# Differential attention with values by head beside queries and keys, one step less in flight, the output projection begun within it, and a first norm that is interleaved

## What is computed

```python
def diff_mixer(h, cos, sin, w_in, lam_vecs, subln_g, w_o, lambda_init):
    q, k, v = jnp.split(h @ w_in, 3, axis=-1)            # 8 heads, 2 x 64 wide; values 128 wide
    q = rope_partial(q.reshape(B, T, H, 2, dh), cos, sin) * (dh ** -0.5)
    k = rope_partial(k.reshape(B, T, H, 2, dh), cos, sin)
    lam = jnp.exp(jnp.sum(lf[0] * lf[1])) - jnp.exp(jnp.sum(lf[2] * lf[3])) + lambda_init
    for i in range(T // Q_BLOCK):                          # 4 blocks of 128 queries
        s = jnp.einsum('bhiqd,bhikd->bhiqk', qb, k[:, :, :, :L])
        p = jax.nn.softmax(jnp.where(mask, s, -jnp.inf), axis=-1)
        a = p[:, :, 0] - lam * p[:, :, 1]
        outs.append(jnp.einsum('bhqk,bhkv->bhqv', a, v[:, :, :L]))
    o = rmsnorm_2(o, subln_g) * (1.0 - lambda_init)
    return o.reshape(B, T, D_MODEL) @ w_o
```

## Time and profile before

| what | us |
|---|---|
| median of 3 runs (lowest, highest) | 2480.9 (2480.77, 2481.79) |
| the profiled execution's own time | 2478.61 |
| its span, first to last instruction | 2476.8 |
| TensorE busy in the span | 2400.5 |
| VectorE busy | 1275.1 |
| ScalarE busy | 821.8 |
| GpSimd busy | 170.0 |
| mean granted clock of TensorE | 0.982 of full speed |

### The profile page before, as it was taken

The page is one execution under the profiler, slowest core; times in us unless marked ns, Lnnn a source line. Parts: engine busy times, 40 slices in busy tenths (PEclk is TensorE's granted clock), DMA queues, the critical chain, the costliest instruction groups (busy, mean ns, idle before and its releaser), DMA issues.

```text
span 2476.8 us, 26889 instructions
## 1 busy us (share of the span) xinstructions
PE 2400.5 (97%) x10944; PEld 1913.9 (77%) x10944; DVE 1275.1 (51%) x1845; ACT 821.8 (33%) x1218; POOL 170.0 (7%) x146
## 2 busy tenths in 40 slices
PE   8999999999999999999999999999998879999998
PEld 6788887877777888887788778888776657888886
DVE  4654544476243455544543466664447773644343
ACT  3322223423433322222543343322333443423221
POOL 0000002021012000001110100000112211000001
PEclk8999999999999999999999999999999989999999
DMA  7756632311112256541232246663141102343330
GB/s 276 248 187 210 195 120 73 97 43 43 60 52 69 85 170 216 193 136 49 94 102 60 69 124 212 209 207 124 38 132 49 43 26 68 118 131 94 97 96 34
DMA packets 80793, 288.06 MB, mean 116 GB/s; under 512 B 8976, under 2 KB 9104, under 8 KB 80672
## 3 DMA queue, kind: packets, MB, share of 16 engines
q1 hardware_dynamic: 79952, 284.78, 36.1%
q10 hardware_dynamic: 720, 1.57, 0.2%
HBM read 284.22 MB, written 2.10 MB: 116 GB/s over the span
## 4 chain that ended last, share of the span: by engine, by line
PE 86%; DVE 8%; ACT 2%; issue 1%; POOL 1%; DMA 1%; SPq 1%; DVEq 0%; ACTq 0%
PE bank L279 23%; PE bank L277 23%; PE bank L278 22%; PE bank L320 2%; PE bank L322 2%; PE bank L321 2%; PE bank L360 1%; PE bank L297 1%; PE bank L302 1%; PE bank L298 1%; PE bank L389 1%; DVE dsm L1856 1%; DVE wlo L1326 1%; PE bank L367 1%; POOL h_sb L1946 1%
## 5 line engine op out<-in xcount | busy, mean ns | idle before, releaser
L1326 DVE TENSOR_TENSOR wlo<-raw,whi 128x1024 fp32r<-128x1024 f32 (+1 forms) x370 | 461.9, 1250 | 464.0 <-ACT whi L829 463.6
L277 PE MATMUL bank<-yhi,whi 128*128 128x512 f32 x1728 | 685.5, 397 | 6.8 <-DVE ylo L1428 3.7
L279 PE MATMUL bank<-yhi,wlo 128*128 128x512 f32 x1728 | 675.1, 391 | 0.0
L278 PE MATMUL bank<-ylo,whi 128*128 128x512 f32 x1728 | 675.1, 391 | 0.0
L829 ACT ACTIVATE whi<-raw 128x1024 fp32r<-128x1024 f32 (+1 forms) x370 | 384.6, 1041 | 359.6 <-PE bank L279 264.6
L277 PEld LDWEIGHTS bank<-yhi,whi 128*128 128x128 f32 x1728 | 326.3, 189 | 82.9 <-issue 10.7
L278 PEld LDWEIGHTS bank<-ylo,whi 128*128 128x128 f32 x1728 | 326.4, 189 | 69.5 <-issue 3.3
L279 PEld LDWEIGHTS bank<-yhi,wlo 128*128 128x128 f32 x1728 | 325.9, 189 | 69.2
L279 PE MATMUL bank<-mlp_ahi,wlo 128*128 128x512 f32 x512 | 204.2, 399 | 0.0
L278 PE MATMUL bank<-mlp_alo,whi 128*128 128x512 f32 x512 | 201.8, 394 | 0.0
L277 PE MATMUL bank<-mlp_ahi,whi 128*128 128x512 f32 x512 | 200.8, 392 | 0.0
(11 more groups left out here) (289 smaller groups left out, 2588.3 us busy)
## 6 DMA issues: line engine op xcount, KB each, us to landing
raw<-in_ada SPq DMA_DIRECT2D x152, 512.0 KB, 4.4
raw<-in_ffn_up SPq DMA_DIRECT2D x88, 512.0 KB, 4.4
raw<-in_mlp_up SPq DMA_DIRECT2D x64, 512.0 KB, 3.6
raw<-in_mlp_dn SPq DMA_DIRECT2D x64, 512.0 KB, 3.7
raw<-in_ffn_dn SPq DMA_DIRECT2D x32, 512.0 KB, 3.9
first<-in_ada SPq DMA_DIRECT2D x16, 512.0 KB, 15.8
raw<-in_w_dqk SPq DMA_DIRECT2D x16, 512.0 KB, 3.7
raw<-in_ffn_dn SPq DMA_DIRECT2D x16, 384.0 KB, 3.6
```

The source lines that it names most:

```text
L277: e.matmul(out, wh, xh[:, kt, :], start=first, stop=False)
L278: e.matmul(out, wh, xl[:, kt, :], start=False, stop=False)
L279: mm = e.matmul(out, wl, xh[:, kt, :], start=False, stop=last)
L1326: e.tensor_tensor(k.wlo[:, what % NW, 0:width], raw[:, 0:width], k.f(k.whi[:, what % NW, 0:width]), ALU.subtract).then_inc(*sig.up("wlo", ...
```

## The change

- **First norm.** TensorE computes only the shifts of tiles 0 and 1 ahead, and `shift(n + 2)` precedes slice n. `four` runs units 0 and 1 over all slices and units 2 and 3 three slices behind. ScalarE and VectorE prepare the first weights one at a time between tiles, VectorE makes two modulation rows ahead instead of three, and its low part follows the scaling of the same tile. SyncE issues weights 0 and 1 in round 1, weight 2 in round 3 and weight 3 in round 4.
- **Projection.** Query, key and value of a head are three feature-major units in a row ("dqkv", 24 units). A value is copied out of its bank, transposed on TensorE (four transposes) and copied again into `dvals`.
- **Steps.** There are 34. The units 4 to 23 are cut into 160 slices, spread evenly over steps 0 to 27, half before and half behind the transposes. A query, key or value is turned one step after its unit ended. The transposes are of step s - 1 and the value product of step s - 2. VectorE combines step s in step s. `dp` and `dsm` have three places. The product with lambda (L1871) becomes a tensor_scalar with the same operand as its scalar.
- **Norms.** Groups of 4, 2 and 2 heads. Heads 0 to 5 are normed and split in steps 28 and 29.
- **Output projection.** Units 24 to 27 begin within the steps: slices 0 to 5 of two of them in steps 29 to 31, of the other two in steps 32 to 35; their slices 6 and 7 follow the norm of heads 6 and 7; then come four whole units.

The core of the diff:

```diff
@@ plan
-            add_units("w_dqk", "dqk", 0, 3)
-            add("w_dv", "dv")
-            add_units("w_dqk", "dqk", 3, 16)
+            add("w_dqkv", "dqkv")
@@ Pe.four
-        for kt in range(NT):
-            before(kt)
-            w.wait_ge(*sig.on(lo, *st, kt))
-            for u, out in zip(us, outs):
-                w.wait_ge(*sig.on("wlo", u))
-                self.three(out, u, kt, xh, xl, kt == 0, kt == NT - 1)
+        for n in range(NT + 3):
+            for kt, at in ((n, 0), (n - 3, 2)):
+                if not 0 <= kt < NT:
+                    continue
+                if at == 0:
+                    before(kt)
+                w.wait_ge(*sig.on(lo, *st, kt))
+                for u, out in zip(us[at:at + 2], outs[at:at + 2]):
+                    w.wait_ge(*sig.on("wlo", u))
+                    self.three(out, u, kt, xh, xl, kt == 0, kt == NT - 1)
@@ Pe.diff
+        self.linear("dqkv", y)
+        turn(0)
+        turn(1)
+        self.linear("dqkv", y)
+        turn(2)
...
+        for s in range(34):
             if s < 32:
+                softmaxes(s, *divmod(s, 4))
+            now = k.d_parts[s]
+            for n, kt in now[:len(now) // 2]:
+                part(n, kt, y if n < 24 else x)
+            for n in k.d_done[s - 1]:
+                turn(n)
+            if 1 <= s < 33:
+                turned(s - 1, *divmod(s - 1, 4))
+            for n, kt in now[len(now) // 2:]:
+                part(n, kt, y if n < 24 else x)
+            if s >= 6 and s % 4 == 2:
+                norm_columns(s // 4 - 1)
+            if s >= 2:
+                values(s - 2, *divmod(s - 2, 4))
+            for h in k.d_spread.get(s, ()):
+                spread(h)
+        for n, kt in k.d_parts[34]:
+            part(n, kt, x)
+        norm_columns(7)
+        for n, kt in k.d_parts[35]:
+            part(n, kt, x)
+        spread(6)
+        spread(7)
+        for n in range(24, 28):
+            for kt in (6, 7):
+                part(n, kt, x)
@@ Dve.diff, in step s
-                e.tensor_tensor(m[:, 7:8], m[:, 7:8], k.lamb[:, 4:5], ALU.mult).then_inc(*sig.up("dcm", s - 1, 1))
+                e.tensor_scalar(m[:, 7:8], m[:, 7:8], k.lamb[:, 4:5], None, ALU.mult).then_inc(*sig.up("dcm", s, 1))
@@ Dve.first_norm
-        for n in range(3):
+        for n in range(2):
             self.ada(1, n)
...
             if n == 0:
-                self.prep_to(3)
-            if n + 3 < NT:
-                self.ada(1, n + 3)
-            if n:
-                low(n - 1)
-        low(7)
+                self.prep_to(0)
+            if n + 2 < NT:
+                self.ada(1, n + 2)
+            low(n)
+            if n < 4:
+                self.prep_to((1, 1, 2, 3)[n])
@@ Sp.program
-            if 1 <= n < 5:
-                e.dma_start(k.raw[:, n - 1, :], k.dram["ffn1_up0"][n - 1]).then_inc(k.s_raw[n - 1], 16)
+            for u in ((), (0, 1), (), (2,), (3,), (), (), ())[n]:
+                e.dma_start(k.raw[:, u, :], k.dram["ffn1_up0"][u]).then_inc(k.s_raw[u], 16)
@@ build_program
+        k.dgroups = [(g, n, n == size - 1) for g, size in enumerate((4, 2, 2)) for n in range(size)]
+        slices = [(n, kt) for n in range(4, 24) for kt in range(8)]
+        k.d_parts = [slices[160 * i // 28:160 * (i + 1) // 28] for i in range(28)]
+        k.d_done = {i: [n for n, kt in part if kt == 7] for i, part in enumerate(k.d_parts)}
+        k.d_done.update({-1: [3], 28: [], 29: [], 30: [], 31: [], 32: [], 33: []})
+        one, two = ([(n + i, kt) for kt in range(6) for i in range(2)] for n in (24, 26))
+        k.d_parts += [[], one[:4], one[4:8], one[8:], two[:3], two[3:6], two[6:9], two[9:]]
+        k.d_spread = {20: (0,), 21: (1,), 22: (2,), 23: (3,), 27: (4,), 28: (5,)}
+        k.d_normed = {28: (0, 1, 2, 3), 29: (4, 5)}
```

More of the change, by code:

```diff
@@ L771, in last_normed, with part @@
-        def last_normed():
-            norm_columns(7)
-            spread(7)
-        x = (k.yhi, k.ylo, "ylo", ("diffx",))
-        self.pair(["do", "do"], x, "yhi", range(8), 7, last_normed)
-        for _ in range(6):
+            self.spread(("dR", h), k.droot_row[g], 4 * n, 16)
+        first = self.u - 4
+        outs = {}
+        def part(n, kt, x=y, kts=8):
+            u = first + n
+            xh, xl, lo, st = x
+            if kt == 0:
+                outs[u] = self.bank("u", u, hold=True)
+            w.wait_ge(*sig.on("wlo", u))
+            w.wait_ge(*sig.on(lo, *st, kt))
+            self.three(outs[u], u, kt, xh, xl, kt == 0, kt == 7)
+            if kt == 7:
+                k.banks.let_go(("u", u))
@@ L778, in diff @@
+        for n, kt in k.d_parts[34]:
[8 more added lines that the diff above has]
+                part(n, kt, x)
+        self.u = first + 28
+        for _ in range(4):
             self.linear("do", x)
@@ L787, in program @@
         self.root("start", 0)
-        for n in (1, 2):
-            self.shift(n)
+        self.shift(1)
         self.ffn("ffn1", FFN_GROUPS, True)
@@ L1206, in diff @@
         e.activation(k.cosr[:, :], kf, F.Sin, bias=k.cst[:, HPI_C:HPI_C + 1], scale=-1.0).then_inc(*sig.up("dtrig", 2))
+        copied(2, self.unit("dqkv"))
         w.wait_ge(*sig.on("dlam", 3))
         e.activation(k.lamb[:, 2:4], k.lamb[:, 0:2], F.Exp).then_inc(*sig.up("dlexp"))
-        for half in range(2):
-            c = slice(512 * half, 512 * half + 512)
-            self.tokens("dv", "dv", 4 * half, lambda j: k.dvals[:, j, c])
-        steps = [(h, i) for h in range(8) for i in range(4)]
@@ new lines, in diff @@
+            if 1 <= s < 33:
+                wd = 128 * ((s - 1) % 4 + 1)
+                w.wait_ge(*sig.on("dturn", s - 1))
+                if s >= 3:
+                    w.wait_ge(*sig.on("dval", s - 3))
+                e.activation(k.daT[:, (s - 1) % 2, 0:wd], k.banks.at("dt", s - 1)[:, 0:wd], F.Copy).then_inc(
+                    *sig.up("daT", s - 1, bank=("dt", s - 1)))
+            for n in k.d_done[s]:
+                copied(n, self.unit("dqkv"))
+            if s == 28:
+                w.wait_ge(*sig.on("lin", k.last["dqkv"]))
+                self.prep_to(k.first["do"] + 3)
@@ L1266, in diff @@
+            for hh in k.d_normed.get(s, ()):
+                self.to_y("diffx", hh, k.dq[:, hh, :], "dn", hh)
+            if s == 18:
+                row_root(0, 3)
+            if s == 26:
+                row_root(1, 5)
+            if s >= 5 and s % 4 == 1:
+                head(s // 4 - 1)
+        row_root(2, 7)
+        for hh in (6, 7):
+            self.to_y("diffx", hh, k.dq[:, hh, :], "dn", hh)
         for n in range(NT):
-            if n >= 2:
-                self.unit("do")
+            self.unit("do")
@@ L1870, in diff @@
+            for n in k.d_done[s]:
+                self.unit("dqkv")
+            if s == 28:
+                self.prep_to(k.first["do"] + 3)
+            if s < 32:
+                m, p = k.dsm[:, s % 3, :], k.dp[:, s % 3, :, :]
+                w.wait_ge(*sig.on("dexp", s, 1))
+                e.reciprocal(m[:, 6:8], m[:, 4:6]).then_inc(*sig.up("dcm", s, 0))
+                w.wait_ge(*sig.on("dcm", s, 0))
                 w.wait_ge(*sig.on("dlam", 5))
-                e.tensor_tensor(m[:, 7:8], m[:, 7:8], k.lamb[:, 4:5], ALU.mult).then_inc(*sig.up("dcm", s - 1, 1))
@@ L1898, in diff @@
+            if s == 26:
+                row_root(1)
+            for hh in k.d_spread.get(s, ()):
+                normed(hh)
+            for hh in k.d_normed.get(s, ()):
+                self.to_y("diffx", hh, k.dq[:, hh, :])
+        row_root(2)
+        for hh in (6, 7):
+            normed(hh)
+            self.to_y("diffx", hh, k.dq[:, hh, :])
         for n in range(NT):
-            self.gated("diff", 0, n, us[n] if n < 2 else self.unit("do"), 17)
+            self.gated("diff", 0, n, self.unit("do"), 17)
```

254 lines of the change are left out of this document (91 added, 163 removed).

## The result

The changed kernel takes 2449.93 us (median of 4 executions: 2446.03, 2446.16, 2453.70, 2453.75), the kernel before, on the same chip, 2480.84 (2476.66 to 2481.79). The ratio is 0.9879, 95% interval 0.9854 to 0.9903: 30.9 us less, by the interval 24 to 36. The forecast was 2465.2, 15.7 less.

The account below looks back on a forecast made before the run. TensorE, 97% busy, bounds; 44 us of attention's idle and slow clock are winnable. 44 - 3.6 (transposes) - 4.9 - 8 - 6.7 - 3.1 - 5 = 12.7, plus 3 at the start: 15.7 won, 2465.2 us, range 2449 to 2478.

Parts of the forecast that it names:

- the first rival: Whole kernel: no chain waits in 28 steps, early clock at start, half the dips absent; 31 us won, chance 0.18.
- Step 4, the uneven chain: The 28 attention steps: chain 6.7 us and TensorE 6.6 are level, so unevenness causes waits; 8 us lost, ends 0 and 20.
- The clock in the stage: Differential attention before the change: lowered TensorE clock costs 12 us; new dips after it cost 5 us.
- The dips at the places named: First rotation, step 29 and tail: long waits pull the clock down; 5 us lost, ends 0 and 8.
- Step 1, the start: First norm: preparing only two units first starts dense work near 27 us, 10 us sooner; 3 us won.
- both cases: At the start: clock stays down until the group of 12, 1.3 us won; or rises at 34 us, 8 us won.
- the clock up before 35 us: At the start: a return of TensorE's full clock before 35 us, listed as showing the forecast wrong.
- the signs of it being right: Under 10 us idle in 28 steps, first-scores wait 4 to 7, output-slice wait about 4, dense work near 27, half clock until 45.
- Steps 3 and 5: First rotation: 4.9 us of new wait; the end: 6.7 us of waits in steps 28 and 32, 3.1 in the tail.
- Step 4's weighing of the Trainium skill: Product with lambda on VectorE: by the skill's rule its tensor_scalar form would wait for GpSimd as the old one does.
- The slower rivals: The 28 steps: 7.2 us each gives 2472, chance 0.16; 7.4 gives 2478, 0.08; 8.0 gives 2494, 0.07.
- The chain as the bound: VectorE in the 20 split steps: steps take 8.0 us, 13 us slower, 2494; decides from 7.5; chance 0.07.

Follow-up runs that it names:

- e6: The changed kernel with a fifth projection unit before the steps, leaving 152 slices instead of 160 in them; 2451.89 us, ratio 0.9885.
- e10: The changed kernel with one more step in flight and four places for the probabilities instead of three; 2452.82 us, ratio 0.9886.
- e12: The changed kernel with VectorE's first two rotations ahead of lambda's last three operations and a weight split; 2450.04 us, ratio 0.9875.
- e5: The changed kernel with the one-element product with lambda a tensor_tensor again; 2452.16 us, ratio 0.9885.
- e8: The changed kernel with the split of the fourth output weight in step 30 instead of 28; 2452.03 us, ratio 0.9887.
- e13: The changed kernel with the first two rotations ahead of lambda's operations and units 2 and 3 two slices behind at the start; 2445.96 us, ratio 0.9861.
- e11: The changed kernel with two full matmuls added between the second and third shift at the start; 2447.16 us, ratio 0.9882.
- e7: The changed kernel with units 2 and 3 of the first norm two slices behind instead of three; 2447.70 us, ratio 0.9879.

## Why the prediction was right and where it was not

The time fell inside the range, 2449 to 2478, by 0.9 us, and two of its four executions lie below it. The forecast was half of the gain. The case that came resembles the first rival, "the cover holds everywhere", priced at 31 us won and 2450. That the median hits this figure is in part luck: the rival takes the early clock at the start as given, and it came in half of the executions, with 8.1 us instead of the rival's 5; the profiled execution, with the late clock, won 24.9.

- **Step 4, the uneven chain, was the wrong term.** 8 us of waits were expected in the 28 steps, and 0.3 us a step for meetings with GpSimd in the chain. From 1816 to 2004 us TensorE is idle for 0.6 us of 188. The estimate of the means was right, as far as the runs show it: a step takes 6.7 us, and 0.2 us less cover (e6) lets waits through. What failed is the inference from level means to waits. By the prediction's sum a step with a split and one without differ by 2.6 us; in the trace combinations follow one another after 4.2 to 9.5 us. But TensorE asks for the combination of a step only behind half of the next step's matmuls, and the margin there (0.14 to 4.0 us) takes up the difference.
- **The clock in the stage was mis-sized.** I took 12 us as the clock's loss before, from two stretches; 0.98 over 203 busy us alone is 4, where I took 2. The whole stage shows 17.0 with 8.4 left (if the idle time is spread evenly over both levels), 8.6 won where 12 - 5 = 7 were forecast. The dips at the places named did come: 0.87 in the stretch that had 0.73.
- **Step 1, the start, was right in its mechanism and its low end, and its value of 3 us holds for one of two groups only.** Dense work began at 26.98 (27 expected) and 0.50 stayed until 48 (some 45); that execution won 3.6. In the others the clock returns early and 11.7 are won (1790.07 to 1778.3), more than the upper end of 8. I had named both cases, and took them for alternatives of the kernel, where they are alternatives of the execution; the median holds something of both. So a sign that was to show the forecast wrong, the clock up before 35 us, stands beside the signs of it being right: it is in the profile of e10, with the same start, while the changed kernel's shows the late clock.
- **Steps 3 and 5 held.** First rotation 4.36 us (4.9). Step 28 and 32: 1.78 + 4.01 + 1.11 = 6.9 (6.7). Tail 1.33 + 1.07 = 2.4 (3.1, of which the 0.7 for the root did not show). But the reason for the first was incomplete: it counted the tables and functions before lambda as the chain, and did not ask whether the rotation needs lambda. It doesn't; it only stood behind it (e12).
- **Step 4's weighing of the Trainium skill.** The trace shows that L1890 did not wait for GpSimd: 214 ns in the mean of 32, six of which began during a GpSimd operation, as at 1930.13 with 0.21 us, while a sum ran from 1929.51 to 1930.78. The prediction had applied the rule of the Trainium skill (SBUF - State Buffer, section "Who interferes with whom") on a tensor_scalar in a two-port mode to it; the section says that such an operation can contend when its operands meet the conditions, and does not speak of one element a partition. The full-width tensor_scalar behind it (L1892) took 0.55 to 1.42 us in four of its six meetings with GpSimd, where 0.35 and 0.42 is usual at these widths (256 and 384); these four are in line with that section. For the time it makes no difference (e5).
- **The slower rivals.** The chain as the bound needed over 7.5 us a step; the steps take 6.7 (187.2 us from 1815.36 to 2002.56 for 28), where 6.6 were forecast without waits.

In the sum of the profiled execution: 15.7 forecast and 24.9 measured. Of the missing 9.2, the uneven chain is 7.4, the start 0.6, the clock in the stage 1.6 and the waits before and behind the steps 1.0; against them stand 1.4 us of other work (5.0 where 3.6 were forecast), and the rest is rounding. To the 30.9 of the medians 6.0 are missing: 2.2 of it is that the execution profiled before lay below the median, the rest that, by their times, half of the executions have the early clock.

## What to carry to other kernels

Two engines with level means do not by themselves make waits; ask by how many matmuls the one that waits lags behind what it waits for, and test it by taking a little cover away, as e6 does. When a wait for a chain seems to be its own length, look at what stands ahead of it on the queue without being needed: three operations and a weight split moved behind the rotations are worth 3.7 us here. When a kernel's executions fall in two groups, take several profiles of the same stretch before pricing it: a mark on the timeline (the first matmul of a later stage) tells in one number which case an execution is.

## What the runs showed of the hardware

- The granted clock returns at different moments in executions with one and the same instruction order at the start: at 30 (e10), 39 (e6, e8) or 48 us (the changed kernel), with no gap on TensorE from 27 us on; the first matmul of differential attention moves by 8.1 us between first and last. In e13 it came back at 30 us and was at half once more from 40 to 44 us (0.57 in the mean).
- Two full matmuls in the middle of the thin stretch did not keep the clock up (e11: 0.50 from 24 to 26 us). Neither they nor a denser order (e7) ended the late executions (2457.92 and 2453.94 us).
- A tensor_scalar of one element a partition was not held beside GpSimd (213 to 216 ns in 32, six of them begun during a GpSimd operation and five wholly inside one). A tensor_tensor of the same shape was, in e5 (0.45 to 1.21 us in six, against 0.16), and a tensor_scalar of 128x384 took 1.42 us against 0.42. With one held operation taken out of the chain, the wait showed in the next.
